# Regrouping the conditioning parts in a two-block transformer kernel on one Trainium2 core

## The chip, the cores and the metric

One core of a Trainium2 chip runs the kernel. The metric is the device time of one execution in microseconds (us), less being better. The engines are TensorE (PE in the profile; its weight loads are PEld), VectorE (DVE), ScalarE (ACT), GpSimd (POOL) and SyncE (SP). Here SP issues nearly all DMAs, and POOL a few. Each engine runs its own instructions in order and waits for the others on semaphores.

## What is computed

Two models run one behind the other, on 256 tokens of width 1024. The first has two layers, and each of its half steps is modulated by vectors that are made from a conditioning vector `c` (and `c_ctx` for the 256 context tokens):

```python
s_c, s_cc = jax.nn.silu(c), jax.nn.silu(c_ctx)
for i in range(DEPTH):                                   # DEPTH = 2
    m  = (s_c  @ ada_w[i] + ada_b[i]).reshape(B, N_MOD, 1, D)   # ada_w[i]: 1024 x 9216
    mc = (s_cc @ ada_w[i] + ada_b[i]).reshape(N_MOD, D)
    x = half_step_ffn(x, m[:, 0], m[:, 1], m[:, 2], ffn_w_in[i, 0], ffn_w_out[i, 0], ...)
    ...                                                  # ctx too in layer 0
    hx = modulate(x, m[:, 3], m[:, 4])
    ...                                                  # layer 0: attention; layer 1: short convolution
    x = post_norm_update(x, y_lat, m[:, 5], 1.0, ...)
    x = half_step_ffn(x, m[:, 6], m[:, 7], m[:, 8], ffn_w_in[i, 1], ffn_w_out[i, 1], ...)
```

The second model (retention, gated recurrence, differential attention, convolutional FFN, two layers) follows and has nothing to do with `ada_w`. All is float32.

## The kernel before

**Weights in chunks.** Every large product is done as a list of steps (`gemm_steps`, L152): `glu` (22 units of 256 columns), `res` (4 units), `v`, `k`, `q` (4 units each), and so on. A unit's weights come in chunks of up to four 128-row tiles, numbered through the whole program by `S`. `glu` of layer 0 is chunks 0 to 43 (two in a unit), `res` is 44 to 67 (six in a unit, the last two of them with three tiles), `v` is 68 to 75 and `k` is 76 to 83. SP loads a chunk into one of four `raw` buffers (L1770), ACT rounds it into `high` (L2068), DVE takes the rest into `low` (L2291), and PE multiplies: three matmuls of 512 columns for each tile and half unit (L1978, L1979, L1980), 24 in a chunk of four tiles.

**Conditioning parts.** `ada_w` is cut into 36 panels of 512 columns, and a panel into four parts `c` of 256 rows. The four first panels come ahead of everything, in buffers `raw0`. The other 128 parts, A = 0 to 127, are spread over the chunks: behind the last matmul of chunk `HOST[A]` PE runs `ada_part` (L1824, called at L1983). A part is 512 KB, loaded by two DMAs of 256 KB (L1775), and is two matmuls of 32 output columns by 512 (L1842), which the profile lists as two instructions each. Their four possible places in the array are chosen by the part's row tile, `h, g = divmod(k, 4)` with `k = 2 * c + y`: parts with even `c` use column groups 0 and 1, those with odd `c` groups 2 and 3.

**Hosts.** `ADA_HOSTS` (L53) has three spans of (first chunk, chunks, parts), and `part_hosts` (L239) spreads the parts of a span evenly. In the first span (chunks 0 to 31, parts 0 to 79) three and two parts stand behind a chunk by turns; in the second (44 to 67, parts 80 to 103) one; in the third (68 to 83, parts 104 to 127) two and one by turns.

**Buffers and the order of loads.** Parts 0 to 79 go round six buffers `part`; 80 to 103 take the buffers `part_sg` (even) and `part_rs` (odd); 104 to 127 take `part_sg` (even) and `part` number 6 (odd). `issue` (L504 to L508) puts the load of part A behind the weight load of chunk `HOST[before] + 4`, where `before` is the part that had the same buffer, and there SP waits until PE has multiplied that part (L1780). SP takes its list in order, so that everything behind such a wait stands still with it. The first load into `part_sg` waits for the last hidden tile of `glu` (L1782).

**Turns.** When 16 parts are done, DVE copies the row (`ada_rows`, L2358), PE turns it into columns (`ada_columns`, L1848, a unit later) and DVE adds the bias. `turn_host` finds the unit in `HOST`.

**POOL's loads.** In the same stretch POOL issues two other transfers: at L2656 a copy of the bias table inside HBM (`rpb_skew`, 3584 KB), as soon as it has scaled `X`, and at L2722 twelve loads of 256 KB from it (`TBZ`), in three batches of four, as units 0, 1 and 2 of `v` have left PSUM.

Of the kernel before, what the change touches and what calls it, by code (L numbers as in the profile page):

```python
# [49 lines left out]
ADA_FIRST = 4  # L50
FIRST_PLACE = (0, 2, 1, 3)
ADA_PARTS = 4 * (ADA - ADA_FIRST)
ADA_HOSTS = ((0, 32, 80), (44, 24, 24), (68, 16, 24))  # L53
NH, HD = 16, 64
GRID_W, GRID_H = 64, SEQ // 64
RH = 4
# [181 lines left out]

def part_hosts():  # L239

    return [S0 + x * n // parts for S0, n, parts in ADA_HOSTS for x in range(parts)]


HOST = part_hosts()


# [2534 lines left out]
```

## Time and profile before

| | |
|---|---|
| Median of 3 runs | 3049.11 us (3046.49 to 3050.3) |
| Span of the profiled execution | 3044.0 us |
| PE busy | 2923.9 us, 96% of the span |
| DVE, ACT, POOL busy | 1757.0, 1380.5, 375.6 us |
| HBM read | 471.23 MB, 156 GB/s over the span |
| Part loads of 256 KB | 184 + 48 + 24, of L1775 |

The span is counted from the first to the last instruction of the profiled execution; the runs are timed from outside and take in what lies around it. A busy PE is not a PE at its peak: matmuls overlap, so that the distance between the starts of two of them, and not the duration shown, tells what one costs. The granted clock (PEclk) is the share of full speed that the chip gave TensorE in a stretch.

### The profile page before, as it was taken

The page shows a single profiled execution, that of the slowest core. Times are in us where ns is not written, and L with a number is a line of the kernel's source. Part 1 is how long each engine was busy: PE and PEld are TensorE (multiplying, and loading weights), DVE is VectorE, ACT ScalarE, POOL GpSimd, SP SyncE. Part 2 cuts the span into 40 slices and gives each one's busy share as a digit, 9 for nine tenths or more (in the row PEclk, how much of TensorE's full clock was granted, in tenths as well). Part 3 has the DMA queues.
Part 4 walks back from the last instruction along what each step waited for, and adds up shares of the span by engine and source line. Part 5 has one row for each costly group of instructions (what it writes and reads, how often), then busy time and mean ns, then how long its engine had stood idle before and what let it go on. Part 6 is the DMA issues. An engine that isn't in the chain of part 4 may idle for free. (4 is left out here: it accounts for less than half of the span.)

```text
span 3044.0 us, 51451 instructions
## 1 busy us (share of the span) xinstructions
PE 2923.9 (96%) x19512; PEld 2567.3 (84%) x19512; DVE 1757.0 (58%) x2624; ACT 1380.5 (45%) x1948; POOL 375.6 (12%) x306
## 2 busy tenths in 40 slices
PE   6999999899999999999899999999999999999998
PEld 3667766677888889888899889799999998988998
DVE  2323224266766657665545865757745577566784
ACT  1222213135655545554453553556644454546663
POOL 2111000123111110111100110101101002020110
PEclk9999999999999999999999999999999999999999
DMA  9886353741565655465435405245545451533563
GB/s 331 281 253 189 114 160 127 194 152 56 165 186 147 193 183 152 147 192 184 133 121 170 146 30 179 84 144 147 170 158 158 142 163 44 156 108 115 156 179 132
DMA packets 586156, 474.80 MB, mean 156 GB/s; under 512 B 28720, under 2 KB 547888, under 8 KB 585664
## 3 DMA queue, kind: packets, MB, share of 16 engines
q1 hardware_dynamic: 584464, 460.44, 49.3%
q0 software_dynamic: 1520, 11.95, 1.3%
q8 instruction: 122, 2.00, 0.3%
q14 instruction: 50, 0.41, 0.0%
HBM read 471.23 MB, written 4.72 MB: 156 GB/s over the span
## 5 line engine op out<-in xcount | busy, mean ns | idle before, releaser
L2291 DVE TENSOR_TENSOR low<-raw,high 128x1024 fp32r<-128x1024 f32 (+1 forms) x744 | 905.6, 1220 | 811.7 <-ACT high L2068 809.3
L2068 ACT CAST high<-raw 128x1024 fp32r<-128x1024 f32 (+1 forms) x744 | 768.3, 1034 | 1001.6 <-PE PS L1980 600.6
L1978 PE MATMUL PS<-NHh,high 128*128 128x272 f32 (+1 forms) x2304 | 669.2, 290 | 14.2 <-DVE NHl L1754 4.7
L1980 PE MATMUL PS<-NHh,low 128*128 128x272 f32 (+1 forms) x2304 | 661.2, 287 | 0.0
L1979 PE MATMUL PS<-NHl,high 128*128 128x272 f32 (+1 forms) x2304 | 660.2, 287 | 0.0
L1978 PEld LDWEIGHTS PS<-NHh,high 128*128 128x128 f32 x2304 | 433.4, 188 | 19.5 <-issue 15.4
L1979 PEld LDWEIGHTS PS<-NHl,high 128*128 128x128 f32 x2304 | 434.0, 188 | 0.8
L1980 PEld LDWEIGHTS PS<-NHh,low 128*128 128x128 f32 x2304 | 433.7, 188 | 0.0
L1976 PE MATMUL PS<-XX,high 128*128 128x512 f32 x966 | 346.8, 398 | 0.0
L1978 PE MATMUL PS<-XX,high 128*128 128x512 f32 (+1 forms) x752 | 273.6, 364 | 3.7 <-DVE XX L2345 2.2
L1975 PE MATMUL PS<-XX,low 128*128 128x256 f32 x966 | 271.2, 281 | 0.3
L1979 PE MATMUL PS<-XX,high 128*128 128x512 f32 (+1 forms) x752 | 266.0, 354 | 0.0
L1980 PE MATMUL PS<-XX,low 128*128 128x512 f32 (+1 forms) x752 | 265.8, 354 | 0.0
L1976 PEld LDWEIGHTS PS<-XX,high 128*128 128x128 f32 x966 | 181.5, 188 | 37.6
L1978 PEld LDWEIGHTS PS<-XX,high 128*128 128x128 f32 x752 | 143.5, 191 | 54.6 <-issue 35.5
L1975 PEld LDWEIGHTS PS<-XX,low 128*128 128x128 f32 x966 | 182.3, 189 | 8.0 <-issue 1.1
L2673 POOL TENSOR_TENSOR GG<-SG,GG 128x256 f32 (+1 forms) x92 | 94.1, 1023 | 729.6 <-ACT GG L2187 639.9
L1980 PEld LDWEIGHTS PS<-XX,low 128*128 128x128 f32 x752 | 143.4, 191 | 20.3
L1979 PEld LDWEIGHTS PS<-XX,high 128*128 128x128 f32 x752 | 143.6, 191 | 17.8
L1976 PE MATMUL PS<-GG,high 128*128 128x512 f32 x420 | 149.4, 398 | 0.0
L1975 PE MATMUL PS<-GG,low 128*128 128x256 f32 x420 | 118.1, 281 | 0.9 <-POOL GG L2673 0.9
L1978 PE MATMUL PS<-OH,high 128*128 128x272 f32 (+1 forms) x384 | 111.7, 291 | 4.6 <-DVEq L2500 4.6
(355 smaller groups left out, 4938.9 us busy)
## 6 DMA issues: line engine op xcount, KB each, us to landing
raw<-w_in_dram SPq DMA_DIRECT2D x416, 256.0 KB, 3.1
raw<-ffn_w_in_dram SPq DMA_DIRECT2D x352, 256.0 KB, 3.4
part<-ada_w_dram SPq DMA_DIRECT2D x184, 256.0 KB, 4.2
raw<-w_ffn_in_dram SPq DMA_DIRECT2D x176, 256.0 KB, 3.2
raw<-ffn_w_out_dram SPq DMA_DIRECT2D x160, 256.0 KB, 3.1
raw<-w_branch_dram SPq DMA_DIRECT2D x96, 256.0 KB, 3.1
raw<-w_ffn_out_dram SPq DMA_DIRECT2D x80, 256.0 KB, 2.9
part_sg<-ada_w_dram SPq DMA_DIRECT2D x48, 256.0 KB, 3.0
```

Of the source, the lines that this page charges most:

```text
L1975: nc.tensor.matmul(out, wl, xh, start=False, stop=False)
L1976: last = nc.tensor.matmul(two, wh, both, start=False, stop=end)
L1978: nc.tensor.matmul(out, wh, xh, start=begin, stop=False)
L1979: nc.tensor.matmul(out, wh, xl, start=False, stop=False)
L1980: last = nc.tensor.matmul(out, wl, xh, start=False, stop=end)
L2068: nc.scalar.copy(high[:, slot, 0:nk, :], raw[:, slot, 0:nk, :]).then_inc(s_high, 1)
L2291: nc.vector.tensor_tensor(low[:, slot, 0:nk, :], raw[:, slot, 0:nk, :], high[:, slot, 0:nk, :].bitcast(F32), ALU.subtract).then_inc(s_low, 1)
L2673: nc.gpsimd.tensor_tensor(out, x, h.bitcast(F32), ALU.subtract).then_inc(s_hl, 1)
```

## The change

Each span of `ADA_HOSTS` gets a fourth number, the group, and `part_hosts` gives all parts of a group the host that the even spread gave its first.

```diff
-ADA_HOSTS = ((0, 32, 80), (44, 24, 24), (68, 16, 24))
+ADA_HOSTS = ((0, 32, 80, 4), (44, 24, 24, 2), (68, 16, 24, 2))
...
-    return [S0 + x * n // parts for S0, n, parts in ADA_HOSTS for x in range(parts)]
+    return [S0 + x // group * group * n // parts for S0, n, parts, group in ADA_HOSTS for x in range(parts)]
```

The hosts are now 0, 1, 3, 4, 6, 8, 9, 11, 12, 14, 16, ... 30 (20 of them, four parts each), 44, 46, ... 66 (12, two each), and 68, 69, 70, 72, 73, 74, 76, 77, 78, 80, 81, 82 (12, two each). Since `issue` and the turns are computed from `HOST`, loads and turns move too.

PE, behind chunks 1 and 2 (`part0_72` to `part5_77` are the six buffers). Before, behind chunk 2:

```order
L1842 MATMUL PS<-part5_77,SCW_68 32x512 x2
L1842 MATMUL PS<-part0_72,SCW_68 32x512 x2
L1842 MATMUL PS<-part1_73,SCW_68 32x512 x2
L1978 MATMUL PS<-XX_61,high_50 128x512
L1979 MATMUL PS<-XX_61,high_50 128x512
```

PE now, behind chunk 1:

```order
L1980 MATMUL PS<-XX_61,low_51 128x512
L1842 MATMUL PS<-part4_76,SCW_68 32x512 x2
L1842 MATMUL PS<-part5_77,SCW_68 32x512 x2
L1842 MATMUL PS<-part0_72,SCW_68 32x512 x2
L1842 MATMUL PS<-part1_73,SCW_68 32x512 x2
```

Parts 5, 6 and 7 stood behind chunk 2; they have moved one chunk ahead, and chunk 2 has none.

SP, at the start of `glu`, from the load of chunks 2 to 4 on. Before:

```order
L1770 DMA raw_49<-ffn_w_in_dram 128x4x128 x6
L1775 DMA part0_72<-ada_w_dram 128x512 x2
L1775 DMA part1_73<-ada_w_dram 128x512 x2
L1775 DMA part2_74<-ada_w_dram 128x512 x2
L1770 DMA raw_49<-ffn_w_in_dram 128x4x128 x2
L1775 DMA part3_75<-ada_w_dram 128x512 x2
L1775 DMA part4_76<-ada_w_dram 128x512 x2
L1770 DMA raw_49<-ffn_w_in_dram 128x4x128 x2
L1775 DMA part5_77<-ada_w_dram 128x512 x2
```

SP now:

```order
L1770 DMA raw_49<-ffn_w_in_dram 128x4x128 x6
L1775 DMA part0_72<-ada_w_dram 128x512 x2
L1775 DMA part1_73<-ada_w_dram 128x512 x2
L1775 DMA part2_74<-ada_w_dram 128x512 x2
L1775 DMA part3_75<-ada_w_dram 128x512 x2
L1770 DMA raw_49<-ffn_w_in_dram 128x4x128 x2
L1775 DMA part4_76<-ada_w_dram 128x512 x2
L1775 DMA part5_77<-ada_w_dram 128x512 x2
L1775 DMA part0_72<-ada_w_dram 128x512 x2
L1775 DMA part1_73<-ada_w_dram 128x512 x2
L1770 DMA raw_49<-ffn_w_in_dram 128x4x128 x4
```

Four part loads now stand together, and then two chunks' loads without any.

SP, in the third span, from the loads of parts 108 and 109 on. Before (the first row is part 108, the last part 113):

```order
L1775 DMA part_sg_79<-ada_w_dram 128x512 x2
L1770 DMA raw_49<-na_w_qkv_dram 128x2x256 x2
L1775 DMA part6_78<-ada_w_dram 128x512 x2
L1775 DMA part_sg_79<-ada_w_dram 128x512 x2
L1770 DMA raw_49<-na_w_qkv_dram 128x2x256 x2
L1775 DMA part6_78<-ada_w_dram 128x512 x2
L1770 DMA raw_49<-na_w_qkv_dram 128x2x256 x2
L1775 DMA part_sg_79<-ada_w_dram 128x512 x2
L1775 DMA part6_78<-ada_w_dram 128x512 x2
```

SP now (parts 108 and 109; 110 and 111; 112 and 113):

```order
L1775 DMA part_sg_79<-ada_w_dram 128x512 x2
L1775 DMA part6_78<-ada_w_dram 128x512 x2
L1770 DMA raw_49<-na_w_qkv_dram 128x2x256 x2
L1775 DMA part_sg_79<-ada_w_dram 128x512 x2
L1775 DMA part6_78<-ada_w_dram 128x512 x2
L1770 DMA raw_49<-na_w_qkv_dram 128x2x256 x4
L1775 DMA part_sg_79<-ada_w_dram 128x512 x2
L1775 DMA part6_78<-ada_w_dram 128x512 x2
```

Part 111 is now asked for beside 110, ahead of the loads of chunks 75 and 76; before it stood between them.

## Rows read from the trace of the kernel before

**Rows 1.** The page: busy time, share of span, instructions of PE.

```profile
PE 2923.9 (96%) x19512; PEld 2567.3 (84%) x19512; DVE 1757.0 (58%) x2624; ACT 1380.5 (45%) x1948; POOL 375.6 (12%) x306
```

**Rows 2.** Waits of PE, 0 to 660 us: total us, times, longest us.

```profile
PE PS L1842 <- DMA raw<-ada_w_dram: 22.7, 4, 11.4
PE PS L1842 <- DMA part<-ada_w_dram: 10.8, 6, 5.7
...
PE PS L1978 <- DVE XX L2327: 1.5, 1, 1.5
```

**Rows 3.** Timeline of PE: start, us, operation; blocks of two and of three parts.

```profile
53.37 0.39 PE L1980 MATMUL PS<-XX,low 128*128 128x512 f32 x1
53.69 1.06 PE L1842 MATMUL PS<-part,SCW 128*32 128x512 f32 x8
...
55.02 0.39 PE L1979 MATMUL PS<-XX,high 128*128 128x512 f32 x1
55.25 0.39 PE L1980 MATMUL PS<-XX,low 128*128 128x512 f32 x1
...
60.36 1.91 PE L1842 MATMUL PS<-part,SCW 128*32 128x512 f32 x12
...
62.54 0.40 PE L1979 MATMUL PS<-XX,high 128*128 128x512 f32 x1
```

**Rows 4.** Timeline of PE: a block of one part, and four first parts together.

```profile
362.30 1.05 PE L1842 MATMUL PS<-part_sg,SCW 128*32 128x512 f32 x4
...
363.62 0.39 PE L1979 MATMUL PS<-GG,high 128*128 128x512 f32 x1
```

```profile
35.39 1.92 PE L1842 MATMUL PS<-raw,SCW 128*32 128x512 f32 x16 [1.99 <-DMA raw<-ada_w_dram]
...
37.58 0.40 PE L1979 MATMUL PS<-XX,high 128*128 128x512 f32 x1
```

**Rows 5.** Start of glu: SP's issues, their landing (parts issued 52.3 to 53.45), POOL, PE.

```profile
50.30 3.15 SPq L1775 DMA_DIRECT2D part<-ada_w_dram  x6
```

```profile
DMA to landing us min/median/max: 4.9/5.5/6.0
```

```profile
61.45 14.33 SPq L1775 DMA_DIRECT2D part<-ada_w_dram  x6
```

```profile
58.51 0.56 POOL L2657 DMA_DIRECT2D rpb_skew<-rpb_dram  x1
```

```profile
rpb_skew<-rpb_dram POOLq DMA_DIRECT2D x1, 3584.0 KB, 16.5
```

```profile
77.45 1.05 PE L1842 MATMUL PS<-part,SCW 128*32 128x512 f32 x4 [1.82 <-DMA part<-ada_w_dram]
```

**Rows 6.** Stretches: us, busy us of PE, PEld, DVE, ACT, POOL, clock, DMA share, GB/s.

```profile
100.00:260.00 160.00, 160.00 (x788) 106.99 (x780) 45.15 (x56) 35.54 (x45) 19.92 (x11) 1.00 0.82 254
...
530.00:562.00 32.00, 25.91 (x102) 16.96 (x101) 8.37 (x7) 4.03 (x4) 6.59 (x8) 0.89 0.82 210
562.00:590.00 28.00, 25.57 (x107) 17.42 (x105) 6.71 (x8) 3.85 (x4) 3.25 (x4) 0.88 0.65 169
```

**Rows 7.** Start of res: PE's first block, SP's issue into part_rs, its landing.

```profile
348.99 1.05 PE L1842 MATMUL PS<-part_sg,SCW 128*32 128x512 f32 x4 [2.45 <-DMA part_sg<-ada_w_dram]
```

```profile
346.40 0.91 SPq L1775 DMA_DIRECT2D part_rs<-ada_w_dram  x2
```

```profile
DMA to landing us min/median/max: 3.6/4.3/5.0
```

**Rows 8.** The third span: PE's two long waits, SP's load of part 111, POOL's second batch.

```profile
552.91 1.92 PE L1842 MATMUL PS<-part,SCW 128*32 128x512 f32 x4 [5.73 <-DMA part<-ada_w_dram]
```

```profile
578.34 1.05 PE L1842 MATMUL PS<-part,SCW 128*32 128x512 f32 x4 [2.43 <-DMA part<-ada_w_dram]
```

```profile
540.55 0.85 SPq L1775 DMA_DIRECT2D part<-ada_w_dram  x2
```

```profile
540.65 3.26 POOL L2722 DMA_DIRECT2D TBZ<-rpb_skew  x4 [4.39 <-DVE NVT L2465]
```

## The prediction

> **What bounds the kernel now.** I read the page first: PE is busy 96% of the span [rows 1], so what counts is what PE has to do and where it stands still. Then the waits of PE over the 660 us in which parts are multiplied: 22.7 us for the first panels, which the change leaves alone, and 10.8 us for `part` buffers [rows 2]. Then PE's timeline around the parts, read by starts: main matmuls start 0.23 us apart (55.02 to 55.25), but a block of parts between them costs more than its own work, since the step from one shape to the other takes 0.32 us (53.37 to 53.69) [rows 3].
>
> **What a block costs.** From the block's start to the second main matmul behind it, plus the 0.32 ahead of it, less the two distances of 0.23 that would be there anyway. Two parts: 55.02 - 53.69 = 1.33, + 0.32 - 0.46 = 1.19 us. Three: 62.54 - 60.36 = 2.18, so 2.04 [rows 3]. One: 363.62 - 362.30 = 1.32, so 1.18 [rows 4]. One costs what two cost, because each fills only two of the four column groups. So four should cost what three cost. The trace has that case once, the four parts of the last first panel: 37.58 - 35.39 = 2.19, so 2.05 [rows 4]. The other bound would be two twos without a joint, 2 x 1.19 = 2.38. I take 2.05, from the row of the same four shapes.
>
> **Span 1 (80 parts).** Before, 16 times a three and a two: 16 x 3.23 = 51.7 us. Now 20 x 2.05 = 41.0. Saved 10.7 us, all on PE's path.
>
> Against it stands the start, where DMAs are behind. The second block (behind chunk 1) now needs parts 6 and 7. SP issues them from 50.30 on in the same place as before, and such loads take 4.9 to 6.0 us to land [rows 5], so part 7 is there at about 57.6. PE comes for it at about 54.0 and leaves at 58.6, where before it went on at about 54.7. Then POOL's table copy: it is issued at 58.51, takes 16.5 us, so until 75.0, and over that time SP's own issues stand still for most of 14.33 us, until 75.8 [rows 5]. POOL's issue does not depend on PE, so it stays where it is. The third block (behind chunk 3, at 69.8) needs part 11, which was late before too (77.45, 1.82 us waited [rows 5]). It is now queued earlier, ahead of two weight chunks, and lands just behind the copy, at about 75.4; chunk 4 ends at about 82. The fourth needs parts 12 to 15. At 254 GB/s for a share of 0.82 [rows 6] the DMAs carry 310 GB/s, 1.7 us for a part, and behind the copy stand part 11, 12, 13, two weight chunks, 14 and 15: until about 85. Chunk 5 then starts at about 85.8, where before it came 2.3 us behind 77.45, at 79.7. That is 6.1 us late although the blocks up to there cost 0.3 less, so **6.4 us of new waiting**. From there on loads keep up: a group's last two parts are asked for when the group before is begun, and in the tightest case, one chunk apart, have 8.4 us. Bounds: 2 us (if part 7 alone costs) and 10 (if the clock falls too). Span 1 gives 10.7 - 6.4 - 1.0 for the clock = **3.3 us**.
>
> The clock is the softest number. After PE's 5.73 and 2.43 us of waiting in `v` [rows 8] it fell: over these stretches it is 0.89 and 0.88 [rows 6], 3.5 and 3.4 us of lost speed. After 2.45 us at 348.99 it did not [rows 7]. So a wait of 3 or 4 us may cost up to 3.4 more, and I put 1.0 for it here. The Trainium skill, "TensorE: Matmul & The Clock Gate", section "HAM oscillation — how this bites in real kernels", says that waits for DMA between groups of matmuls throttle the clock again each time. By that each of the two late blocks would lose 3.4 us and span 1 would come out at about -2. The trace agrees for two waits and not for the third.
>
> **Span 2 (24 parts).** Before 24 ones: 24 x 1.18 = 28.3 us. Now 12 twos: 14.3. Saved 14.0. Each pair has two chunks (over 8 us) to be loaded, so no wait in the run of it. But the first block now needs part 81 too, whose second DMA is issued at about 346.8 and takes 5.0 us: 351.8, and PE goes on at 352.8 where before it did at 350.0 [rows 7]. Minus 2.8: **11.2 us** (8 to 13, the lower end with a fallen clock).
>
> **Span 3 (24 parts).** Before 16 blocks at 1.19, now 12: saved 4.8. Here POOL's table loads collide with SP's. Before, part 111 was asked for at 540.55, beside the second batch at 540.65, and came 12 us later; PE stood 5.73 us, and once more 2.43 at 578.34 [rows 8]. In the two stretches PE was idle 6.1 and 2.4 us and lost 3.5 and 3.4 us to the clock [rows 6]: 15.4 us in all. Now 111 is issued with 110 at 533.5 and used two chunks later, at 544.5, in time. But 112 and 113 are issued at 545.6, behind the second batch, and used one chunk later, at 551.3. Counting what is queued from 533 on (two batches, four parts, two chunks) at the pace of before puts 113 at about 556: some 4.7 us idle, and 3.5 for the clock. The third batch comes with the end of chunk 73, about 553 instead of 564, and meets parts 114 and 115, used at about 563: 2 us idle and 2 for the clock. Together 12.2 us, 3.2 less than before. Bounds: none at all, if the loads slip between the batches, and 25, if both hops are late by as much as the worst of before. I take 12 because the same data goes through the same queue. Span 3: 4.8 + 3.2 = **8.0 us**.
>
> **Turns.** Column products that stood right behind a block stand alone in four places; each pays the step between shapes once more, at most 0.2 us by the 0.32 against 0.23 [rows 3]. Minus 0.8. DVE's row copies move with their blocks by at most a unit; DVE is busy 45 of 160 us there [rows 6], which hides them. The rest of the program is the same.
>
> **Sum.** 3.3 + 11.2 + 8.0 - 0.8 = 21.7 us. The span of 3044.0 becomes 3022.3; the median of the runs stands 5.1 above that span, and 3049.1 - 21.7 = **3027.4 us**.
>
> **Rivals.**
> - *The table loads collide worse.* Both hops behind chunks 72 and 73 are late by what 5.73 us was before, with the clock: 24 us instead of 12.2. For it: two parts now hang on one chunk's time. Against: 110 and 111 get out of the way. Gain 10, time 3039.
> - *The collision is gone.* 112 to 115 land in time. For it: 110 and 111 are early. Gain 21.7 + 12 = 34, time 3015.
> - *Groups of four do not share the array* and cost 2.38: 20 x 0.33 = 6.6 less, time 3034. Rows 4 speak against it.
> - *SP's loads are not held by POOL's copy.* The Trainium skill, "DMA: Bandwidth & Descriptors", section "Issuing engines are not separate DMA queues", says that DMAs of all issuers interleave on the same 16 engines. As a mechanism here: the parts would come through between 62 and 75 at about half the pace, the start would lose 3 instead of 6.4, time 3024. The 14.33 us of SP [rows 5] speak against it.
> - *Slower: one-chunk hops are late everywhere.* In 8 of 20 groups of span 1 and 8 of 12 of span 3 the next loads have one chunk. A late hop costs what 578.34 did, 2.4 + 3.4 = 5.8 us. From four more of them on the gain is gone; six give 3027 + 35 = 3062. For it: in span 3 there is no slack beyond the chunk's 5.5 us, and two parts need about that. Against: DMAs are busy 0.82 in span 1 with no wait [rows 6], and would go to about 0.88.
> - *The regrouping changes nothing to speak of*, since PE's lead is given back to a later wait: 3049. PE has hardly any later wait in these 660 us [rows 2], so this is small.
>
> **Chances.** Forecast and what lies within some 6 us of it (with the skill's copy rival) 0.60; collision worse 0.13; collision gone 0.12; no sharing 0.05; nothing 0.05; slower 0.05. The range takes in the worse and the milder collision and their bounds: 3012 to 3041. About 0.2% (6 us) is what a measurement here can tell from no change: faster by more 0.90, within 0.05, slower 0.05.
>
> **What would show it.** PE's blocks of 16 instructions with 2.19 us to the second main matmul (the wrong end: 2.5). In `res`, blocks of two at 1.33 behind every second chunk, and the first one leaving at about 352.8 less what was saved before. Waits of PE for `part` of some 4 us each at about 55 and 72, and after 85 none before `res`. In `v`, the 5.73 us wait moved from the block behind chunk 72 to that behind 73, and POOL's third batch some 10 us sooner after the second. The forecast is wrong if blocks of four are longer than threes, if waits show up regularly between 100 and 260 us, or if the clock falls at more than two or three places before 650 us.

## The result, and the profile after

| | median us | runs | profiled execution's span |
|---|---|---|---|
| before | 3047.80 (3044.93 to 3050.30) | 4 | 3044.0 |
| changed | 3027.73 (3026.50 to 3029.82) | 4 | 3028.0 |

The ratio of the changed kernel to the one before is 0.9943, with a 95% interval of 0.9930 to 0.9957: a gain of 17 us, between 13 and 21. (The ratio is the steadier number; the medians alone would say 20.) A second timing on another chip, beside nine runs of the kernel before, gave 0.9942 (0.9929 to 0.9956).

First the page of the changed kernel, the line that answers to [rows 1]:

```profile
PE 2906.7 (96%) x19512; PEld 2569.8 (85%) x19512; DVE 1758.1 (58%) x2624; ACT 1380.8 (46%) x1948; POOL 375.1 (12%) x306
```

The instructions are the same in number, and PE is busy 17.2 us less. So nearly all of the gain is in busy time, and waiting did not become less. The waits of PE from 0 to 660 us (total, times, longest), against [rows 2]:

```profile
PE PS L1842 <- DMA raw<-ada_w_dram: 21.5, 4, 11.3
PE PS L1842 <- DMA part<-ada_w_dram: 9.2, 10, 3.4
PE PS L1842 <- DMA part_sg<-ada_w_dram: 5.0, 2, 2.6
...
PE PS L1842 <- DMA part_rs<-ada_w_dram: 1.4, 1, 1.4
```

Before, PE stood 13.2 us for parts behind the first panels (10.8 and 2.4); now it is 15.6 us, in thirteen shorter waits. What the blocks themselves cost stands in PE's timeline (start, us, operation; in brackets what it waited before and for what), one block of four in the middle of `glu`:

```profile
134.48 0.39 PE L1980 MATMUL PS<-XX,low 128*128 128x512 f32 x1
134.80 1.92 PE L1842 MATMUL PS<-part,SCW 128*32 128x512 f32 x16
136.65 0.50 PE L1978 MATMUL PS<-XX,high 128*128 128x512 f32 x1
136.99 0.40 PE L1979 MATMUL PS<-XX,high 128*128 128x512 f32 x1
```

From its start to the second main matmul 136.99 - 134.80 = 2.19 us, the very time that [rows 4] had for the first four parts, and 0.32 ahead of it as in [rows 3]: 2.05 us as a price. The rest of PE's timeline shows where the waiting is. The start of `glu`, behind chunks 1, 3 and 4:

```profile
55.23 1.06 PE L1842 MATMUL PS<-part,SCW 128*32 128x512 f32 x8
58.01 1.05 PE L1842 MATMUL PS<-part,SCW 128*32 128x512 f32 x4 [1.71 <-DMA part<-ada_w_dram]
59.36 1.05 PE L1842 MATMUL PS<-part,SCW 128*32 128x512 f32 x4 [0.30 <-DMA part<-ada_w_dram]
...
71.47 1.92 PE L1842 MATMUL PS<-part,SCW 128*32 128x512 f32 x16
...
79.56 1.05 PE L1842 MATMUL PS<-part,SCW 128*32 128x512 f32 x4 [0.47 <-DMA part<-ada_w_dram]
80.99 1.05 PE L1842 MATMUL PS<-part,SCW 128*32 128x512 f32 x4 [0.37 <-DMA part<-ada_w_dram]
85.44 1.05 PE L1842 MATMUL PS<-part,SCW 128*32 128x512 f32 x4 [3.40 <-DMA part<-ada_w_dram]
86.83 1.92 PE L1842 MATMUL PS<-part,SCW 128*32 128x512 f32 x4 [0.34 <-DMA part<-ada_w_dram]
88.68 0.80 PE L1978 MATMUL PS<-XX,high 128*128 128x512 f32 x1
```

A group whose parts come one by one loses twice: the waits, and the overlap, since each part then costs its own 1.05 us (79.56, 80.99, 85.44, 86.83) where four together cost 1.92. The block behind chunk 4 takes 9.1 us instead of 1.9. The last two rows are matmuls with the clock down (0.80 from 84 to 88 us, 0.77 from 88 to 92). SP's queue and POOL's copy there, against [rows 5]:

```profile
56.89 5.05 SPq L1775 DMA_DIRECT2D part<-ada_w_dram  x8
61.99 16.49 SPq L1770 DMA_DIRECT2D raw<-ffn_w_in_dram  x4
78.53 5.76 SPq L1775 DMA_DIRECT2D part<-ada_w_dram  x8
```

```profile
61.69 0.56 POOL L2657 DMA_DIRECT2D rpb_skew<-rpb_dram  x1
```

The copy is issued at 61.69, 3.2 us later than before, takes 16.5 us again, and over that time SP gets four issues out. The parts of the fourth block (12 to 15) are asked for from 78.53 on, and PE comes for the first of them at 79.1. The start of `res`, against [rows 7]:

```profile
347.87 1.05 PE L1842 MATMUL PS<-part_sg,SCW 128*32 128x512 f32 x4 [2.39 <-DMA part_sg<-ada_w_dram]
350.37 1.92 PE L1842 MATMUL PS<-part_rs,SCW 128*32 128x512 f32 x4 [1.44 <-DMA part_rs<-ada_w_dram]
352.22 0.80 PE L1978 MATMUL PS<-GG,high 128*128 128x512 f32 x1
```

And `v`, behind chunks 73 and 74, with POOL's second and third batch of table loads, against [rows 8]:

```profile
545.76 1.05 PE L1842 MATMUL PS<-part_sg,SCW 128*32 128x512 f32 x4 [2.56 <-DMA part_sg<-ada_w_dram]
547.16 1.90 PE L1842 MATMUL PS<-part,SCW 128*32 128x512 f32 x4 [0.35 <-DMA part<-ada_w_dram]
...
558.09 1.05 PE L1842 MATMUL PS<-part,SCW 128*32 128x512 f32 x4 [1.60 <-DMA part<-ada_w_dram]
```

```profile
532.65 3.25 POOL L2722 DMA_DIRECT2D TBZ<-rpb_skew  x4 [6.06 <-DVE NVT L2465]
545.24 3.24 POOL L2722 DMA_DIRECT2D TBZ<-rpb_skew  x4 [9.35 <-DVE NVT L2465]
```

The three stretches, columns as in [rows 6], of the changed kernel:

```profile
70.00:100.00 30.00, 25.43 (x110) 15.85 (x109) 6.35 (x8) 6.04 (x8) 1.53 (x1) 0.94 0.98 309
340.00:366.00 26.00, 22.17 (x89) 14.96 (x87) 5.77 (x7) 4.57 (x6) 1.54 (x1) 0.87 0.42 131
530.00:590.00 60.00, 55.49 (x249) 37.97 (x248) 16.39 (x17) 8.87 (x9) 8.33 (x9) 0.97 0.81 223
```

and of the kernel before:

```profile
70.00:100.00 30.00, 27.95 (x129) 17.92 (x131) 8.70 (x9) 7.52 (x10) 3.62 (x2) 1.00 1.05 343
340.00:366.00 26.00, 23.55 (x101) 16.61 (x100) 6.99 (x8) 4.87 (x6) 1.54 (x1) 1.00 0.47 148
530.00:590.00 60.00, 51.48 (x207) 34.38 (x205) 15.08 (x15) 7.88 (x8) 9.84 (x12) 0.89 0.74 191
```

In the first two the changed kernel idles more and runs at a lower clock; in the third it idles 4.5 us instead of 8.5 and loses 1.8 us to the clock instead of 6.6.

One place serves below as a milestone: the first matmul of the attention, where all 128 parts are done. In PE's timeline, before and changed:

```profile
670.36 1.13 PE L1597 MATMUL PS<-NK,NQ 64*128 64x512 f32 x4
```

```profile
651.45 1.13 PE L1597 MATMUL PS<-NK,NQ 64*128 64x512 f32 x4
```

There the changed kernel is 18.9 us ahead, of which 9.7 at the block behind chunk 68 (519.04 before, 509.37 now). At the end 16.0 are left; the last 350 us ran at 0.97 instead of 0.98 in this execution.

### The profile page after: what moved, and what is told of

Same layout as the page of the kernel before. It is cut to its first block and busy times, and to the rows that moved or that the text cites. A ratio compares the mean times of both kernels' runs of the same rounds, so it can differ in the third digit from the quotient of the medians.

```text
span 3028.0 us, 51451 instructions
## 1 busy us (share of the span) xinstructions
PE 2906.7 (96%) x19512; PEld 2569.8 (85%) x19512; DVE 1758.1 (58%) x2624; ACT 1380.8 (46%) x1948; POOL 375.1 (12%) x306
```

## The experiments

The edits are against the changed kernel unless the text says otherwise. Chips differ by some us, so each run is read against the runs of the kernel before that it shares a chip with.

**Each span alone.** The three runs regroup one span, and leave the others one by one.

```diff
-ADA_HOSTS = ((0, 32, 80, 4), (44, 24, 24, 2), (68, 16, 24, 2))
+ADA_HOSTS = ((0, 32, 80, 4), (44, 24, 24, 1), (68, 16, 24, 1))    # e1_span1
+ADA_HOSTS = ((0, 32, 80, 1), (44, 24, 24, 2), (68, 16, 24, 1))    # e2_span2
+ADA_HOSTS = ((0, 32, 80, 1), (44, 24, 24, 1), (68, 16, 24, 2))    # e3_span3
```

> Only the first span is grouped (80 parts in fours); the other two are spread as before. Theory (the blocks' own price, less the late start): blocks of four at 2.05 us against 16 x 3.23 before save 10.7 us, and the start up to chunk 5 gives back 6 to 9 of it, with a fallen clock: 0 to 4 us faster than before, the ratio between 0.9985 and 1.000. Rival (the change's gain is all there, and the start's loss is only this profile's cold first panels): 9 to 11 us faster, ratio 0.9965.

> Only the second span is grouped (24 parts in twos behind every second chunk). Theory: 12 blocks of 1.18 us are gone, 14 us, and the first block gives back 2.8 (waiting for part_rs) plus what the clock then loses, seen as 3.4 at most in the changed kernel: 8 to 11 us faster, ratio 0.9965 to 0.9974. Rival (the clock's loss belongs to the shifted moment, not to the second wait): 11 to 14 us faster.

> Only the third span is grouped (24 parts in twos). Theory: 4 blocks of 1.19 us less, and the waits and the clock behind POOL's table loads fall from 15.4 us to about 10: 8 to 10 us faster, ratio 0.9967 to 0.9974. Rival (the collision is as long, it only moved): 5 us faster, ratio 0.9984.

| | median us | ratio to before (3046.94) | gain | attention begins |
|---|---|---|---|---|
| span 1 | 3040.61 | 0.9974 (0.9964 to 0.9984) | 8 (5 to 11) | 666.17 |
| span 2 | 3034.77 | 0.9956 (0.9939 to 0.9972) | 13 (9 to 19) | 659.66 |
| span 3 | 3041.36 | 0.9981 (0.9970 to 0.9993) | 6 (2 to 9) | 666.44 |

All three gain, the second most, as the sum had it. By the times they give 27 us, more than the whole change's 17. Their intervals are 3 to 5 us wide on each side; taken together with that of the change this makes some 8 us (an estimate), so that a difference of 10 is at the edge of what chance gives, and it stays open whether the spans take something from each other. By the milestone the three add up, 4.2 + 10.7 + 3.9 = 18.8 us against 18.9 for the whole change, but that is worth little: each is one execution, and the one traced for span 1 was the slowest of its eight (3046.97 us, the median 3040.61). Span 1 came out between its two expectations; its interval of 5 to 11 us leaves out the theory (0 to 4) and takes in the rival (9 to 11), while its trace has the late start that the theory spoke of, with a wait of 4.0 us behind chunk 3.

**What sets a block's price.** [Rows 4] said that four parts cost what three do. The reading was that a part fills two of the four column groups. First the order inside a group of four: the two parts of the lower pair of column groups, then the two of the upper, instead of alternating. (For this a load waits until PE has done the whole group that used its buffer.)

```diff
-                        for A in ada_parts(S + c):
+                        here = ada_parts(S + c)
+                        if len(here) == 4:
+                            here = [here[0], here[2], here[1], here[3]]
+                        for A in here:
```

> The changed kernel with each group of four multiplied in the order first, third, second, fourth, and its buffers asked for again only when the whole group is done. Neighbours then share their two column groups, but for the second and third. Theory (a block of four is short because neighbours sit in different column groups): three rounds of 0.85 us instead of two, so 3.0 us from the block's start to the second main matmul instead of 2.2, and with 20 blocks some 17 us slower than the changed kernel. Rival (the block is short for another reason, the switch of shapes alone being saved): 2.2 as before and the time unchanged.

The block did not change. PE's timeline:

```profile
132.68 1.94 PE L1843 MATMUL PS<-part,SCW 128*32 128x512 f32 x16
134.54 0.50 PE L1979 MATMUL PS<-XX,high 128*128 128x512 f32 x1
134.88 0.40 PE L1980 MATMUL PS<-XX,high 128*128 128x512 f32 x1
```

2.20 us against 2.19; the median was 3031.55 us, 0.9948 (0.9931 to 0.9965). That neighbours in the order must lie in different column groups is wrong. Then the same sixteen instructions with other parts: each group of four uses one pair of column groups only, all other things alike.

```diff
+ORDER = ((0, 0), (0, 2), (1, 0), (1, 2), (0, 1), (0, 3), (1, 1), (1, 3))
...
+def part_of(A):
+    if A >= 80:
+        return ADA_FIRST + A // 4, A % 4
+    n, c = ORDER[A % 8]
+    return ADA_FIRST + 2 * (A // 8) + n, c
...
-                load_ada(parts_at[slot], s_part[slot], ADA_FIRST + A // 4, A % 4)
+                load_ada(parts_at[slot], s_part[slot], *part_of(A))
```

> The changed kernel with the 80 parts of the first span taken in another order: each group of four holds parts of one pair of column groups alone (row tiles 0, 1, 4, 5 of two panels, then 2, 3, 6, 7 of them), so that two column groups carry twice the matmuls and two carry none. Theory (a block lasts as long as the fullest column group takes, whatever the order in it): four rounds of two passes at 0.43 us where there are two, so some 3.9 us from the block's start to the second main matmul instead of 2.2, and 20 blocks make it some 34 us slower than the changed kernel, about 3062. Rival (the engine keeps four such matmuls going wherever they sit): 2.2 us and no change.

```profile
137.40 3.63 PE L1851 MATMUL PS<-part,SCW 128*32 128x512 f32 x16
140.95 0.50 PE L1987 MATMUL PS<-XX,high 128*128 128x512 f32 x1
141.29 0.40 PE L1988 MATMUL PS<-XX,high 128*128 128x512 f32 x1
```

3.89 us instead of 2.19, 1.70 more in each of the 20 blocks. The kernel takes 3051.17 us, 1.0029 (1.0019 to 1.0040) times the one before on the same chip: the whole gain is gone and more. It is 9 us slower than before, so some 26 slower than the change, where 20 x 1.70 = 34 were to be paid. The gap lies at the start: the block behind chunk 6 begins at 97.95, 2.4 us sooner than in the change (100.34), although the four blocks ahead of it cost 6.8 us more. There the longer blocks fill time in which the change waits, loses the overlap of its parts or has a lower clock (1.00 against 0.94 from 70 to 100 us). So the fullest column group sets a block's price, whatever the order, and filling all four alike is what makes a group of four worth its while.

**POOL's table copy at the start.** The copy into `rpb_skew` is needed only in `v`. It is put behind hidden tile 17 of `glu`, near 300 us, once in the kernel before and once in the changed one.

```diff
-            pool.dma_start(rpb_skew, bass.AP(rpb_d.tensor, 0, [[0, GRID_W], [RPB_W, NH * 7], [1, RPB_W]])
-                           ).then_inc(s_skew_out, 16)
...
+                            if s is steps[0] and u == 17:
+                                pool.dma_start(rpb_skew, bass.AP(rpb_d.tensor, 0,
+                                                                 [[0, GRID_W], [RPB_W, NH * 7], [1, RPB_W]])
+                                               ).then_inc(s_skew_out, 16)
```

> The kernel before, with POOL's copy of the bias table (3584 KB) issued at about 300 us, behind the hidden tile of unit 17 of glu, instead of at 58. Theory (the copy holds up SP's loads): no wait of PE for parts behind chunks 4 and 5, 2 to 5 us faster than before, ratio 0.9985 to 0.9993. Rival (the start is short of bandwidth whatever POOL does): same as before.

> The changed kernel with the same late copy. Theory (the late start of the grouped span is the copy's doing): the two waits of 3 to 5 us behind chunks 3 and 4 and the clock's fall after them are gone, 5 to 8 us faster than the changed kernel, about 3021. Rival (groups of four are late at the start anyway, since SP's part loads must catch up): no more than 2 us faster than the changed kernel.

The kernel before hardly notices: 3040.69 against 3042.22 us, 0.9992 (0.9981 to 1.0002). The wait of 1.82 us [rows 5] is gone, and from the block behind chunk 2 to the one behind chunk 8 it takes 42.6 us (63.29 to 105.93) instead of 45.9 (60.36 to 106.26), so some 3 us in the trace and 2 in the times, the latter not told from nothing. The same stretch takes 43.3 and 47.7 us in the traces that regroup only span 2 and only span 3, both with the copy where it was, so the 3 us may be anything from 1 to 5. In the changed kernel it is worth 0.9928 (0.9917 to 0.9940) instead of the 0.9942 and 0.9943 of the change alone, 3018.61 us. The stretch that answers to 25.43 busy us and a clock of 0.94:

```profile
70.00:100.00 30.00, 30.00 (x155) 20.61 (x153) 9.70 (x10) 7.31 (x9) 3.35 (x2) 1.00 0.84 256
```

The waits behind chunk 4 are gone, and the four chunk loads that SP issued in 16.49 us beside the copy now take a third of that:

```profile
62.41 5.35 SPq L1770 DMA_DIRECT2D raw<-ffn_w_in_dram  x4
```

The block behind chunk 6 comes at 92.45 instead of 100.34, 7.9 us sooner. From the block behind chunk 1 to the one behind chunk 6 the seven traces with this first span and the early copy take 42.5 to 45.1 us, and two with the late copy 36.9 and 38.3, so 4 to 8 us are the copy's. By the ratios the late copy gives 4.4 us, which is less than the widths of their intervals and alone not told from nothing; it lies between the two expectations (5 to 8, and 2 at most). (At the milestone, 642.20, it is 9.3 ahead of the change, but the traced execution was the fastest of its six.) What is left at the start are 0.60 us behind chunk 0 and 1.83 and 0.29 behind chunk 1, where the copy is not yet issued in the change.

**The first pair of `res`.** Second span one chunk later, so that parts 80 and 81 have another chunk to land.

```diff
-ADA_HOSTS = ((0, 32, 80, 4), (44, 24, 24, 2), (68, 16, 24, 2))
+ADA_HOSTS = ((0, 32, 80, 4), (45, 24, 24, 2), (68, 16, 24, 2))
```

> The changed kernel with the pairs of the second span one chunk later (behind chunks 45, 47, ... 67). Theory (the first pair stands for its two loads, and then the clock falls): PE no longer waits at the start of res, 3.8 us of waiting, 0.9 for two parts multiplied apart and 3.4 of clock go, so 6 to 8 us faster than the changed kernel, about 3021, less 0.6 for a block ahead of the column product at the end of the step. Rival (the wait is only moved behind chunk 45): 0 to 2 us faster.

The first pair now runs in full overlap and without a wait:

```profile
347.67 0.62 PE L1842 MATMUL PS<-part_sg,SCW 128*32 128x512 f32 x2
347.69 0.62 PE L1842 MATMUL PS<-part_rs,SCW 128*32 128x512 f32 x2
348.13 0.60 PE L1842 MATMUL PS<-part_sg,SCW 128*32 128x512 f32 x2
```

```profile
340.00:366.00 26.00, 26.00 (x122) 19.65 (x121) 5.79 (x7) 3.76 (x4) 1.27 (x1) 1.00 0.63 194
```

PE is busy for all 26 us at the full clock, where the change had 22.17 and 0.87: 3.8 us idle and 3.4 of clock. The kernel takes 3015.61 us, 0.9916 (0.9903 to 0.9928), about 8 us better than the change by the ratios.

**The change once more, and the third span spread out.** First the changed kernel unaltered, to see how far one execution lies from another; then the pairs of the third span where the next loads have time before POOL's batches.

```diff
+    hosts = [...]
+    for x, S in enumerate((68, 69, 70, 72, 74, 76, 77, 78, 79, 80, 81, 82)):
+        hosts[104 + 2 * x:106 + 2 * x] = [S, S]
+    return hosts
```

> The changed kernel once more, beside the three that follow. All theories: 0.9943 of the kernel before, within 0.993 to 0.9957.

> The changed kernel with the twelve pairs of the third span behind chunks 68, 69, 70, 72, 74, 76 and then every chunk to 82 (before: 72, 73, 74, 76, 77, 78, 80, 81, 82). Theory (the pairs behind 73 and 74 stand for loads that are queued beside POOL's table loads and have one chunk to land): with two chunks the 4.5 us of waiting, 1.7 for parts multiplied apart and 1.7 for the clock go, 6 to 8 us faster than the changed kernel, about 3021. Rival (the third batch of table loads follows the end of chunk 73, so that with no wait behind 72 it comes sooner and the pairs are late behind 74 and 76 instead): 0 to 3 us faster.

The change again: 3024.87 us, 0.9942 (0.9929 to 0.9956), the first attention matmul at 646.53 instead of 651.45. So the same kernel's milestone moves by 5 us from one execution to the next, and a difference of that size between two traces, at the milestone, says nothing. The spread version takes 3015.13 us, 0.9915 (0.9901 to 0.9929), 8 us less, and shows no wait for a part in its third span:

```profile
530.00:590.00 60.00, 60.00 (x290) 43.09 (x289) 20.97 (x20) 11.49 (x12) 8.47 (x9) 1.00 0.83 236
```

POOL's batches are as close as in the change (12.8 us from the second to the third, there 12.6). It was not their nearness that cost, but that two pairs were to be loaded beside them within one chunk each.

**All together.** The late copy, the second span from chunk 45 and the spread third span in one kernel; then with the first groups behind chunks 0, 2, 3, 5 and 6 as well.

```diff
+    for x, S in enumerate((0, 2, 3, 5, 6)):
+        hosts[4 * x:4 * x + 4] = [S] * 4
```

> Late copy, second span one chunk later, and the third span spread, all three on the changed kernel. Theory (three separate losses): 8 + 8 + 7 us less the little that they share, 3004 to 3010. Rival (what one gives the next takes, as PE comes earlier to the same loads): 3012 to 3016, no better than the best of them alone.

> The same with the first groups of four behind chunks 0, 2, 3, 5, 6 instead of 0, 1, 3, 4, 6. Theory (the second group waits for parts 6 and 7, whose loads are issued in the same place as before): 2 to 4 us faster than the kernel with the three changes. Rival (the DMAs are short of bandwidth up to 90 us, and the wait moves to the next group): the same.

The first takes 3003.23 us, 0.9866 (0.9851 to 0.9881), and waits for parts only behind chunks 0 and 1 (2.2 us in all). The second takes 2998.75 us, **0.9853 (0.9838 to 0.9868)**, 45 us less than the kernel before, and begins the attention at 625.73. Its waits for parts and its stretches:

```profile
PE PS L1847 <- DMA part<-ada_w_dram: 0.9, 2, 0.6
```

```profile
70.00:100.00 30.00, 30.00 (x157) 21.38 (x150) 9.46 (x11) 6.42 (x8) 3.37 (x2) 1.00 0.95 300
340.00:366.00 26.00, 26.00 (x124) 18.78 (x123) 7.74 (x10) 5.88 (x6) 0.54 (x1) 1.00 0.64 202
530.00:590.00 60.00, 60.00 (x292) 42.00 (x291) 26.33 (x23) 12.04 (x13) 3.44 (x4) 1.00 0.76 227
```

It does the change's work with all its late loads mended, and that takes the gain from 17 to 45 us. Not all of the step was lost by the regrouping: the kernel before had waits and a lower clock in the same places too (1.82 us [rows 5], 2.45 [rows 7], and in `v` 8.5 us idle and 6.6 of clock). Of the three mendings only the late copy was tried without the regrouping, so how much the other two would give the kernel before is not shown. The last 4.5 us between the two rest on overlapping intervals.

## Why the prediction held, and where its terms were off

The forecast of 3027.4 us meets the median of 3027.7, but better than its sum deserves. The sum took 21.7 us off the 3049.1 known then. The runs beside the changed kernel put the one before at 3047.8, and the ratio says 17 us (13 to 21). So the sign, the three sources and the order of their sizes were right, and the sum was some 4 us too large.

**Block prices: right.** Two parts 1.19, four 2.05. The second was taken from the one block of four that the trace had and was met to 0.01 us. The reason given, column groups, is what decides (3.89 us where only two of them were used). That four must cost what three cost follows from it: 1.92 us is two parts' work in the fuller pair of groups.

**The start: size right, places wrong in this execution.** The prediction had waits of about 4 us at 55 and 72. The block behind chunk 1 took 5.1 us (55.23 to 60.34) where 4.6 were forecast, but only 2.0 of them were waits; 1.9 are what a block of four takes anyway, and the rest is lost overlap. The block behind chunk 3 did not wait at all, and the second loss fell on the one behind chunk 4, with 4.6 us of waits, the lost overlap, and the clock. The step that failed is "POOL's issue does not depend on PE, so it stays where it is". The copy came 3.2 us later: half of that from the scaling of `X` ahead of it beginning at 46.15 instead of 44.64, the rest from each scaling taking longer. That beginning does follow PE: it is 7.4 us behind PE's first main matmul in the trace before, in the changed kernel's and in the one with the shifted second span (37.24 and 44.64, 38.75 and 46.15, 36.88 and 44.30). So parts 8 to 11 slipped through ahead of it, and 12 to 15 stood behind it. Chunk 5 began at 88.68, 9.0 us later than before, where 6.1 were forecast. Of the rest, 1.5 is a late start that has nothing to do with the change: PE waited for the same first panels, but worked at a granted clock of 0.53 from 20 to 40 us, and in the kernel before at 0.91. The run with the shifted second span has the same first span, and its trace had the full clock there (1.00 from 20 to 40 us). Its start went as forecast:

```profile
57.80 0.56 POOL L2657 DMA_DIRECT2D rpb_skew<-rpb_dram  x1
```

The forecast had 58.51 for this copy. PE then waited 2.7 us behind chunk 1, 2.0 behind chunk 3 and 0.5 behind chunk 4, and chunk 5 began at 86.05, where 85.8 were forecast. And in the run that regroups span 1 alone the copy came at 60.06, and the long wait (4.0 us) stood behind chunk 3. So what failed is that the first 40 us, and with them the copy's moment, were taken to be alike in every execution. That the copy holds the loads up is shown by the late copy (4 to 8 us in the regrouped kernel). In the kernel before, the same copy cost some 3 us (1 to 5), so part of the price of the regrouping was probably that of a copy that had been cheaper; the two ranges touch. As to the whole span: chunk 32 starts 1.1 us ahead of before (273.5 against 274.6), 2.6 without the late start, where the sum had 3.3.

By the Trainium skill, "DMA: Bandwidth & Descriptors", section "Issuing engines are not separate DMA queues", DMAs of different issuers interleave and the issuer does not matter. In the measured case they did interleave, but SP's four issues took 16.49 us beside one copy and 5.35 without it, so interleaving was no protection; the rival built on that rule (a loss of 3 us) did not come about.

**The start of `res`: under-sized.** 2.8 us were put down for a second wait; the loss was 5.1 (the first two pairs lie 17.2 us apart, without a wait 12.1). Missing were the overlap, since the parts came apart and cost 1.05 each, and the clock. "11.2 us (8 to 13, the lower end with a fallen clock)" was therefore its own lower half: 14.0 - 5.1 = 8.9, and the milestone gives 9.7 - 1.1 = 8.6 between chunk 32 and chunk 68.

**The third span: moved as said, milder than said.** The 5.73 us wait did move from the block behind chunk 72 to that behind 73, and POOL's third batch came 12.6 us after the second instead of 23.5. But the waits were 2.9 and 1.6 us and the clock 1.8, together 6.3 where 12.2 were forecast. The step that failed is taking the pace of before for what is queued: from 530 to 590 us DMAs moved 223 GB/s, before 191. That this pace is the whole cause is argued and not shown; in other traces with the same third span the waits were 3.3 us (the change again) and 6.4 (late copy, and second span shifted). Of the 4.8 + 8.8 = 13.6 us that this would give, 9.2 arrived at the milestone, 0.8 went on turns, and some 3.6 I can't place; two executions of the changed kernel lie 4.9 us apart there.

**The clock** is where the prediction was softest. With a second wait right behind the first (2.39 and 1.44 us) it fell to its lower level; PE's stretches behind the pair at 350.37:

```profile
350.00:354.00 4.00, 3.63 (x8) 1.68 (x9) 0.96 (x1) 0.83 (x1) 0.00 (x0) 0.50 0.65 197
354.00:358.00 4.00, 4.00 (x15) 3.17 (x14) 0.00 (x0) 0.00 (x0) 0.00 (x0) 0.74 0.89 288
```

0.50 is 1.2 GHz instead of 2.4. Before, a single wait of 2.45 us [rows 7] left it at 1.00 over 340 to 366 us; with the same single wait of 2.4 us it was 0.93 there in the run that regroups span 3 alone. So one wait of that length can go either way. The Trainium skill, "TensorE: Matmul & The Clock Gate", section "HAM oscillation — how this bites in real kernels", says that DMA waits between groups of matmuls throttle the clock each time. The traces agree for the start of `res` and for the long waits behind chunk 4 in `glu`, not for the 2.0 us behind chunk 1 (1.00 from 40 to 60 us), and for the third span only in part (0.94 from 530 to 560 in one execution of the changed kernel, 1.00 in another).

**The rivals.** Collision gone and collision worse both lost to a milder collision; groups that don't share the array: refuted for these groups, and true when their parts share column groups; one-chunk hops late everywhere: refuted. From 100 to 260 us PE is busy for all 160 us at a DMA share of 0.85 (forecast 0.88):

```profile
100.00:260.00 160.00, 160.00 (x823) 111.90 (x822) 49.89 (x58) 36.58 (x46) 20.93 (x12) 1.00 0.85 264
```

**Still open:** how the 27 us of the single spans fit the 17 of the whole (the difference is at the edge of chance), what each span is worth to better than some us, and the 3.6 us above.

## What to carry to other kernels

Small matmuls that use only some column groups are best done in groups that fill all four alike: one switch of shape is paid for the lot, and the fullest group sets the price. Before grouping them, look for each group at when its last operand is asked for and what else is in the DMAs then, on every issuer's queue: a group that is one load short costs the wait, the overlap and perhaps the clock. The places where a regrouping creates waits are few and visible in a trace (in more than one, since they move from execution to execution), and mending them (another chunk, another moment for an unrelated copy) brought more here than the regrouping alone (from 17 to 45 us), though part of it the kernel before could perhaps have had as well.

## What the hardware showed that I had not expected

- Matmuls of free column groups do not queue behind those of a busy one. With two parts of the same column groups in a row, and two of the others behind them, the sixteen instructions took 1.94 us as before; taken strictly in order they would have had to take about 2.8 (the second pair of groups could start only after 0.9). The pair at 347.67 shows it directly: the second part's first instructions start 0.02 us behind the first part's, and the first part's second pass 0.44 us later. The Trainium skill, "TensorE: Matmul & The Clock Gate", section "The mechanism", says that matmuls start and end in program order; the starts here don't agree, and the measurement decides (the ends are modelled in a profile and say nothing). The trace shows it by the semaphores on which the parts' first weight loads wait, one for each buffer: in the block at 132.67 of the run with the other order the four parts, in the order in which the code has them, begin at 132.67, 133.13, 132.70 and 133.16 us, so the third ahead of the second. In the block at 55.41, where the second part's load was late, the second begins ahead of the third (56.902 and 56.915). The order is thus settled while the kernel runs. So it does not hold for PE's small matmuls that each engine runs its instructions in order, as the first section has it.
- Beside a single copy from POOL of 3584 KB four of SP's issues took 16.49 us, and 5.35 without it; it cost some 3 us in the kernel before (1 to 5) and 4 to 8 in the regrouped one.
- The clock in the first 40 us differs between executions without any change to the work there: 0.91 and 0.53 from 20 to 40 us, and 1.00 in the run with the shifted second span. Where it was down (0.50 to 0.83) POOL's copy came at 60.1 to 61.7 us, otherwise (0.91 and 1.00) at 58.5 and 57.8.
